# Token factors applied after the projections, and constant matmuls in four waits of TensorE

## The reference, cut to what matters

```
def rms_norm(x, g):
    y = xf * lax.rsqrt(jnp.mean(xf * xf, axis=-1, keepdims=True) + EPS)
    return (y * g.astype(jnp.float32)).astype(x.dtype)

def conv_ffn(h, w_up, conv_w, conv_b, w_down):      # h = rms_norm(x, g)
    gu = h @ w_up
    g, u = gu[..., :D_FF], gu[..., D_FF:]
    g = conv(g, conv_w) + conv_b                     # causal, width 3, per feature
    return (jax.nn.silu(g) * u) @ w_down

# keys and values: rms_norm(x, norm_kv) @ kv_w; queries: rms_norm(x, norm_mix[1]) @ w_q
```

## Time and profile before

| | |
|---|---|
| median of 3 runs | 2296.23 us (2291.31 to 2297.32) |
| the profiled execution | 2288.34 us, span in the profile 2286.5 us |
| PE busy | 2167.1 us (95%) |
| DVE, ACT, POOL busy | 56%, 33%, 30% |
| mean granted clock of PE | 0.963 |
| glu tiles on PE | until about 257 us |
| up and down of layer 0 | to 642 us |
| keys, values, queries | 650 to 788 us |
| stick-breaking attention, wo | 793 to 958 us |
| up and down of layer 1 | to 1335 us |

### The profile page before, as it was taken

One profiled execution on the slowest core, in us unless ns is written; L12 is line 12 of the kernel. 1 busy time (PEld: TensorE's weight loads), 2 busy tenths in 40 slices (PEclk: granted clock), 3 DMA queues, 4 the chain that ended last, 5 costly groups with the idle time before them and its releaser, 6 DMA issues. The chain is left out here.

```text
span 2286.5 us, 27572 instructions
## 1 busy us (share of the span) xinstructions
PE 2167.1 (95%) x10821; PEld 1584.2 (69%) x10821; DVE 1282.6 (56%) x2330; ACT 754.4 (33%) x1091; POOL 695.6 (30%) x436
## 2 busy tenths in 40 slices
PE   8859899999999999999999999999999999999898
PEld 7858688888868766778888855436875446886663
DVE  8562389984363267278882032348763574225872
ACT  3422333222243476332232131325651332332210
POOL 6614344445435500344444410011000342441000
PEclk9979899999989999999999989998999979999999
DMA  4032244434434500234443320130002213322201
GB/s 180 7 54 86 74 141 144 147 119 133 123 92 125 129 1 1 83 115 150 141 138 92 92 116 25 56 74 21 2 1 93 92 67 132 96 92 92 74 19 74
DMA packets 54096, 199.69 MB, mean 87 GB/s; under 512 B 9929, under 2 KB 10105, under 8 KB 48751
## 3 DMA queue, kind: packets, MB, share of 16 engines
q1 hardware_dynamic: 37440, 148.53, 20.7%
q0 software_dynamic: 12800, 48.23, 6.5%
q10 hardware_dynamic: 3728, 1.18, 0.3%
HBM read 179.04 MB, written 10.49 MB: 83 GB/s over the span
## 5 line engine op out<-in xcount | busy, mean ns | idle before, releaser
L1505 POOL TENSOR_TENSOR w_lo<-raw,w_hi 128x1024 fp32r<-128x1024 f32 (+1 forms) x216 | 513.8, 2379 | 854.8 <-ACT w_hi L1138 854.6
L595 PE MATMUL psum<-h_hi,w_hi 128*128 128x512 f32 x1216 | 487.6, 401 | 7.3 <-ACT h_hi L1145 5.5
L596 PE MATMUL psum<-h_hi,w_lo 128*128 128x512 f32 x1216 | 479.5, 394 | 0.0
L1138 ACT ACTIVATE w_hi<-raw 128x1024 fp32r<-128x1024 f32 (+1 forms) x216 | 224.9, 1042 | 605.8 <-PE psum L600 395.4
L600 PE MATMUL psum<-h_lo,w_hi 128*128 128x512 f32 x1216 | 303.3, 392 | 0.0
L595 PEld LDWEIGHTS psum<-h_hi,w_hi 128*128 128x128 f32 x1216 | 231.0, 190 | 71.3 <-ACT h_hi L1145 14.2
L600 PEld LDWEIGHTS psum<-h_lo,w_hi 128*128 128x128 f32 x1216 | 230.5, 190 | 48.5
L596 PEld LDWEIGHTS psum<-h_hi,w_lo 128*128 128x128 f32 x1216 | 231.9, 191 | 45.8 <-issue 0.2
L464 PE MATMUL psum<-big,ring 128*128 128x512 f32 x480 | 209.1, 594 | 0.0
L464 PEld LDWEIGHTS psum<-big,ring 128*128 128x128 f32 x480 | 90.9, 190 | 113.9 <-issue 112.6
L642 PE MATMUL psum<-f_hi,w_hi 128*128 128x512 f32 x352 | 137.6, 391 | 0.0
(11 more groups left out here) (384 smaller groups left out, 3388.2 us busy)
## 6 DMA issues: line engine op xcount, KB each, us to landing
raw<-in_ffn_w_up SPq DMA_DIRECT2D x88, 512.0 KB, 3.7
raw<-in_ffn_w_down SPq DMA_DIRECT2D x32, 512.0 KB, 3.6
raw<-in_hy_in SPq DMA_DIRECT2D x32, 512.0 KB, 3.5
ffn_buf<-in_ada_w POOLq DMA_DIRECT2D x20, 512.0 KB, 5.0
sq<-in_ada_w POOLq DMA_DIRECT2D x20, 512.0 KB, 5.1
raw<-in_ssm_w_glu SPq DMA_DIRECT2D x16, 512.0 KB, 3.7
spec<-big SPq DMA_DIRECT2D x8, 1024.0 KB, 3.9
big<-spec POOLq DMA_DIRECT2D x8, 1024.0 KB, 5.1
```

Of the source, the lines that this page charges most:

```text
L595: pe.matmul(o, hi[:, k, :], h_of(k), start=k == 0, stop=False)
L596: pe.matmul(o, lo[:, k, :], h_of(k), start=False, stop=False)
L1138: act.activation(w_hi[:, (n % 2) * HALF:(n % 2) * HALF + w], raw[:, (n % 4) * HALF:(n % 4) * HALF + w], ACT.Copy).then_inc(S["w_hi"], 1)
L1505: pool.tensor_tensor(w_lo[:, at:at + w], raw[:, (n % 4) * HALF:(n % 4) * HALF + w], w_hi[:, at:at + w].bitcast(F32), ALU.subtract).then_in ...
```

## The change

The three norms ffn0, kv and ffn1 are taken apart. ACT writes the high part of gain times X as soon as a row of X is there (`gained`), and its square (`row`); DVE writes the low part (`rest`). The projection runs on these without the token factor. PE sums the squares of rows 0 to 6 ahead of the first tile, those of row 7 in the middle of tile 0, and spreads the factor in the middle of tile 1 (`factor`, `mid`). The factor R is then multiplied in where the results are read: the gate branch (into `ZR`), the down tiles (`DOWN_R`, then added to X), keys and queries (`KQ`), values (`R_COL`). In the up part ACT now waits for DVE's multiplication before it writes the base of the convolution; the high part of the gate moves from DVE to ACT (`gate_hi`), the low part one step later (`gate_lo`). In the last glu step the order of a split and the sigmoid is changed. The buffers move: ada blocks 20 to 27 now lie in `ffn_buf` rather than `Hb`, their loads wait until the last gate is done, and stand behind the third chunk of a down tile rather than the first. `keep_clock` adds matmuls of constants: 8 before `scores(0)`, 3 before the sums of norm nw0, and 3 before each of the spreads of final, nw0 and final2.

```diff
-        ADA_ISSUE = [{2 * j: j for j in range(ADA_UP)} | {2 * FT + 3 * m: ADA_UP + m for m in range(KT)},
+        ADA_ISSUE = [{2 * j: j for j in range(ADA_UP)} | {2 * FT + 3 * m + 2: ADA_UP + m for m in range(KT)},
...
-                Hb[:, (j % 2) * HALF:(j % 2 + 1) * HALF]
+                ffn_buf[:, (j % 2) * HALF:(j % 2 + 1) * HALF]
...
+            def keep_clock(n, bank=None):
+                b = turn[0] % 8 if bank is None else bank
+                if n and last_release[b]:
+                    pe.wait_ge(*last_release[b])
+                for _ in range(n):
+                    pe.matmul(psum[:, b, 0:256], mat("ident"), mats[:, 0:256], start=True, stop=True)
+
+            def sums(name, ks):
+
+                o = take(pe, ("norm", name)) if ks[0] == 0 else ps(("norm", name))
+                for k in ks:
+                    pe.wait_ge(S["sq_ready"], n_sq[0] + 1)
+                    n_sq[0] += 1
+                    for j in range(4):
+                        i = pe.matmul(o[32 * j:32 * j + 32, 0:P], mat("ones")[:, 0:32],
+                                      sq_of(name, k)[:, j * P:(j + 1) * P], start=k == 0, stop=k == KT - 1,
+                                      skip_group_check=True)
+                    if name == "kv" and k < KT - 1:
+                        i.then_inc(S["sq_used"], 1)
+                if ks[-1] == KT - 1:
+                    fills(i, ("norm", name))
+
+            def factor(name):
+                def mid(t):
+                    if t == 0:
+                        sums(name, (KT - 1,))
+                    if t == 1:
+                        if name == "kv":
+                            o = take(pe, ("rc", name))
+                            pe.wait_ge(S["rn_ready"], WIDE_NORMS.index(name) + 1)
+                            fills(pe.transpose(o[:, 0:P], rows_of(name), mat("ident")), ("rc", name))
+                        spread(name)
+                return mid
...
             def norm(name):
 
                 src, n, m, _ = norm_src(name)
+                keep_clock(3 if name == "nw0" else 0)
...
-                norm(f"ffn{l}")
+                sums(f"ffn{l}", range(KT - 1))
...
+                    if mid:
+                        mid(t)
...
                         ada_turn(j)
+                    if l == 0 and m == 4:
+                        sums("kv", range(4))
...
+                    keep_clock(8, 7)
                     pe.wait_ge(S["masks_ready"], 2)
...
+            def gained(name, k):
+                act.activation(H_PARTS[name][0][:, k, :], X[:, k, :], ACT.Copy, scale=col(name, k)).then_inc(S["h_hi"], 1)
+
+            def row(name, k):
+                x_wait(k)
+                gained(name, k)
+                if name == "kv" and k >= 4:
+                    act.wait_ge(S["sq_used"], n_used[0] + k - 3)
+                act.activation(sq_of(name, k), X[:, k, :], ACT.Square).then_inc(S["sq_ready"], 1)
+
+            def root(name):
+                act.preload_act_table_set("sqrt_and_others")
+                act.wait_ge(*full(("norm", name)))
+                frees(act.activation(rows_of(name), ps(("norm", name))[:, 0:P], ACT.Sqrt, bias=eps, scale=1.0 / D),
+                      ("norm", name))
+                n_x[0] += 8
+                n_used[0] += 7 * (name == "kv")
...
-                for n in (2 * m + 2, 2 * m + 3):
-                    split_hi(n)
+                split_hi(2 * m + 2)
+                if m < 7:
+                    split_hi(2 * m + 3)
                 if m >= 2:
                     act.wait_ge(*free(("glu", 2 * (m - 2))))
                 evac(("glu", 2 * m + 1), scr[:, (m % 2) * L:(m % 2 + 1) * L], func=ACT.Sigmoid)
+                if m == 7:
+                    split_hi(2 * m + 3)
+                if m:
+                    row("ffn0", m - 1)
+            row("ffn0", 7)
...
-                    act.wait_ge(*full((f"up{l}", 2 * m)))
-                    act.activation(CONVG[:, m % 2, :], ps((f"up{l}", 2 * m)), ACT.Identity,
+                    act.wait_ge(*free((f"up{l}", 2 * m)))
+                    act.activation(CONVG[:, m % 2, :], ZR[:, m % 2, :], ACT.Identity,
                                    bias=col(f"conv{l}", 3 * FT + m), scale=col(f"conv{l}", 2 * FT + m)) \
                         .then_inc(S["conv_base"], 1)
                     split_hi(n0 + 2 * m + 2)
+                    if m >= 2:
+                        gate_hi(m - 2)
                     if m >= 1:
                         silu(m - 1)
                     split_hi(n0 + 2 * m + 3)
+                gate_hi(FT - 2)
                 silu(FT - 1)
+                gate_hi(FT - 1)
...
                 if j == ADA_UP:
-                    pool.wait_ge(*full(("up0", 2 * FT - 1)))
+                    pool.wait_ge(S["lo_done"], FT)
...
+            def rest(name, k):
+                hi, lo = H_PARTS[name]
+                dve.wait_ge(S["h_hi"], SPLIT_AT[name] + k + 1)
+                STT(lo[:, k, :], X[:, k, :], col(name, k), hi[:, k, :].bitcast(F32), ALU.mult, ALU.subtract) \
+                    .then_inc(S["h_lo"], 1)
...
+                    if factor:
+                        if m:
+                            dve.wait_ge(S["x_ready"], factor + m)
+                        step(TT(DOWN_R, ps(key), R, ALU.mult))
+                        own()
+                        i = TT(X[:, m, :], DOWN_R, X[:, m, :], ALU.add)
...
+            def factor(name):
+                inv_rms(name)
+                if name == "kv":
+                    frees(dve.tensor_copy(R_COL, ps(("rc", name))[:, 0:P:32]), ("rc", name))
+                keep_r(name)
+                dve.wait_ge(*free(("rb", name)))
...
                 for m in range(FT):
                     key = (f"up{l}", 2 * m)
-                    g, z = CONVG[:, m % 2, :], ps(key)
-                    dve.wait_ge(S["conv_base"], FT * l + m + 1)
+                    g, z = CONVG[:, m % 2, :], ZR[:, m % 2, :]
                     dve.wait_ge(*full(key))
-                    step(STT(g[:, 1:L], z[:, 0:L - 1], col(f"conv{l}", FT + m), g[:, 1:L], ALU.mult, ALU.add))
-                    own()
-                    frees(STT(g[:, 2:L], z[:, 0:L - 2], col(f"conv{l}", m), g[:, 2:L], ALU.mult, ALU.add), key)
-                    if m >= 1:
-                        gate(m - 1)
+                    if m >= 2:
+                        dve.wait_ge(S["conv_done"], FT * l + m - 1)
+                    frees(TT(z, ps(key), R, ALU.mult), key)
                     if m < ADA_UP:
                         if m >= 2:
                             ada_reduce(ADA_UP1 * l + m - 2)
                         ada_sum(ADA_UP1 * l + m)
+                    dve.wait_ge(S["conv_base"], FT * l + m + 1)
+                    step(STT(g[:, 1:L], z[:, 0:L - 1], col(f"conv{l}", FT + m), g[:, 1:L], ALU.mult, ALU.add))
+                    own()
+                    STT(g[:, 2:L], z[:, 0:L - 2], col(f"conv{l}", m), g[:, 2:L], ALU.mult, ALU.add) \
+                        .then_inc(S["conv_done"], 1)
+                    if m >= 1:
+                        gate(m - 1)
+                    if m >= 2:
+                        gate_lo(m - 2)
+                gate_lo(FT - 2)
                 gate(FT - 1)
+                gate_lo(FT - 1)
```

More of the change, by code:

```diff
@@ L1246, in ffn @@
                     split_hi(n0 + 2 * m + 3)
+                gate_hi(FT - 2)
                 silu(FT - 1)
+                gate_hi(FT - 1)
                 for n in range(n0 + 2 * FT + 2, n0 + HALVES):
                     split_hi(n)
+                    m = (n - n0 - 2 * FT) // 3
+                    if l == 0 and (n - n0 - 2 * FT) % 3 == 2 and m:
+                        row("kv", m - 1)
             ffn(0)
-            norm("kv", ready=x_wait, then=HALVES_AT["k"])
-            split_rows("kv")
+            split_hi(HALVES_AT["k"])
+            row("kv", 7)
+            split_hi(HALVES_AT["k"] + 1)
+            root("kv")
             for t in range(8):
-                key = ("k", t)
                 split_hi(HALVES_AT["k"] + t + 2)
-                split_rows("mix1", (t,), QHI)
-                act.wait_ge(*full(key))
+                gained("mix1", t)
+                act.wait_ge(*free(("k", t)))
                 for h in (2 * t, 2 * t + 1):
-                    act.activation(KS[half(h), h, :], ps(key)[half(h), :], ACT.Copy).then_inc(S["ks_hi"], 1)
+                    act.activation(KS[half(h), h, :], KQ[t % 2][half(h), :], ACT.Copy).then_inc(S["ks_hi"], 1)
             for q in range(8):
@@ L1300, in _ @@
                 split_hi(HALVES_AT["wo"] + t + 2)
-            n_x[0] += 8
+                if t:
+                    row("ffn1", t - 1)
+            split_hi(HALVES_AT["ffn1"])
+            row("ffn1", 5)
+            row("ffn1", 6)
+            split_hi(HALVES_AT["ffn1"] + 1)
+            row("ffn1", 7)
             ffn(1)
@@ L1965, in _ @@
                         own()
+            for t in range(8):
+                dve.wait_ge(*full(("k", t)))
+                if t >= 2:
```

(6 more changed lines are left out.)

183 lines of the change are left out of this document (96 added, 87 removed).

## The result

The change makes the kernel slower: 2388.38 us (median of four runs, 2385.30 to 2390.34) against 2293.77 (2290.16 to 2297.32), a ratio of 1.0411, 95% interval 1.0389 to 1.0434. I had forecast 2312, slower, with a range up to 2330. The direction is right, the size is not: +94.6 us where the sum had +15.9. The time of before is taken anew beside each experiment and lies between 2291.8 and 2293.8, so a difference between two groups of runs is good to about 2 us.

The account below looks back on a forecast made before the run. PE, busy 95% of the span, was taken as the bound. Gains of 28.7 us against a down-tile loss of 44.6 gave +15.9 on 2296.2, so 2312.1 us, range 2276 to 2330.

Parts of the forecast that it names:

- The direction: Whole kernel: slower, chance 0.66, against same 0.14 and faster 0.20.
- the sum: Whole kernel: loss of 44.6 us less gains of 28.7, so +15.9 us.
- The up tiles of layer 0: Up pairs: base, split and `w_lo` one DVE multiplication later, covered by DVE's slack; cost 0, up to 22 us without cover.
- rival 4: Up tiles: DVE's multiplication over 0.5 us late, PE waits up to 0.5 in 44 pairs; 2334 us, chance 0.06.
- The last sentence of the prediction: Prediction is wrong if L623 has no idle, or if even up tiles wait for `w_lo` all along.
- The down tiles of layer 0: Ada loads 9.1 us later: eight PE waits before the ada transposes, 32.6 us plus 12.0 of clock, loss 44.6.
- Rival 3: Down tiles of layer 0: every wait paid at half clock, loss 51.8 us, total +23.1, 2319 us; chance 0.15.
- kv: Norm before keys and values: cost falls from 15.6 to 4.5 us, gain 11.1.
- ffn1: Norm ahead of layer 1's up tiles: gain 6.6 us, or 4.2 after 2.4 of clock loss.
- The new wait at up tile 2: Tile 2's split stands behind the base, which waits for R: PE idles 4.0 us in ffn0 and in ffn1.
- ffn0: Norm ahead of layer 0's up tiles: tile 2 starts at 276.8, gain 10.0 us, or 7.6 after clock loss.
- Constant matmuls: They fill PE's waits at the opening and nw0: gains 3.3 us (0 to 6.2) and 2.5 us (0 to 5.2).

Follow-up runs that it names:

- the thinned kernel: Changed kernel with seven of eight products left out of the ada sums beside layer 0's up tiles: 2320.20 us.
- The fastest kernel: Changed kernel with product in PSUM, ada loads 21 to 27 early, next even tile's split ahead of R in every pair, sums between convolution and gate: 2262.75 us.

## Why the prediction was wrong, step by step

- **The up tiles of layer 0: cost 0, cover VectorE's slack.** This is the step that failed. I counted the durations of single instructions, found that VectorE loses a CAST and gains a shorter multiplication, and gave 0, at most 22 us (rival 4). I followed what waits for what, and left out what runs beside what: the sums, moved ahead of the convolution, began just before the split, and a split of 2.40 us became one of 5.3. The stretch is 76 us longer than the sum had it, and thinning the sums gives 68.2 back. Without them a cost near 0 was right: with the longer way to the split and the product in place, the thinned kernel loses 0.2 us a pair. The last sentence of the prediction named the sign, even up tiles that wait for `w_lo` all along, and that is what came. The rows to see it with were there. In the kernel before, the CAST reads and writes SBUF and takes 1.48, from 328.98 to 330.46, where the split beside it ends at 330.18; where no split runs beside it the same CAST takes 0.50 in that very trace, and it took 0.45 at the end of a split in the kernel before with its sums moved. I took 1.48 for its length and booked it as relief. And the multiply-adds of `ada_sum` in down tile 1 took 5.35 where an undisturbed chain takes 3.76, with a split inside it.

The Trainium skill, "SBUF — State Buffer", section "Who interferes with whom", states such a rule: a VectorE instruction with two SBUF inputs, or a copy, cast or `tensor_scalar` in a 2-port mode, and a GpSimd instruction that reads SBUF take one lock, and whichever is second stands still for the other's whole instruction. The runs agree, 2.40 to 5.32 on one side and 0.75 to 2.72 on the other, and no stall of a multiply-add with an input in PSUM. They go beyond it in one point: a split that was second waited not for one instruction of 0.34 us but for the rest of the dense chain (the table above).

- **The down tiles of layer 0: +44.6.** Right in place, number and total. Eight waits of 31.0 us where 32.6 stood; the traces give +46 for the stretch. Undoing the shift of seven loads gives 36.2: 27.3 of waits and 8.9 of clock (12.3 by the traces), 1.3 to 1.8 a wait, where I had 12.0 for all eight. The delay of the load minus the margin of each tile was the right working. How the waits spread over the tiles was wrong: I had more in the first four, whose sums have 16 instructions, and less in the last four with 8. They are 3.7 in each of the first four and 4.6, 4.6, 4.6 and 2.5 in the last. The seven multiply-adds there let the split in and stand still for it, one of them for 2.3 us instead of 0.35:

```profile
689.69 4.25 DVE L1957 SCALAR_TENSOR_TENSOR ffn_buf<-ffn_buf,small 128x128 f32<-128x128 f32 x6
...
690.68 2.34 POOL L1599 TENSOR_TENSOR w_lo<-raw,w_hi 128x1024 fp32r<-128x1024 f32 x1 [1.68 <-ACT w_hi L1193]
```

- **Rival 3, every wait paid at half clock.** At this case's 2.4 each that is 16.8 for the seven waits, and 8.9 to 12.3 came. The Trainium skill, "TensorE: Matmul & The Clock Gate", section on HAM oscillation, by which each round of such a loop starts throttled, holds here in part: the clock fell in the down tiles (0.91), but the price was lower.
- **kv: -11.1.** The traces give -11.5.
- **ffn1: -4.2.** The traces give -4.7 for all of layer 1's ffn. The new wait at up tile 2 is 4.08 us, predicted 4.0.
- **ffn0: -7.6, wait of 4.0 at up tile 2.** The wait is 6.67, and tile 2 starts at 280.28 and not at 276.8, against 286.8 before. Of the 2.7 above the forecast, 2.3 are the same fault: with the sums behind the gate the wait is 4.37. The wait itself, an order of ScalarE's queue, was read rightly: with the split ahead of the wait for R it is gone in both layers, though tile 4 takes over a part of it in layer 0 (2.5) and layer 1 (1.5).
- **Constant matmuls: -3.3 and -2.5.** Together they bring 3.6 by the comparison without them, which is not clear of noise. The norms give 1.9; at the opening the traces show 0.4, so there the bound of half the clock's loss was no guide and the lower bound, 0, was nearer.
- **The total without the three faults.** By the prediction's terms the gains without both waits at tile 2 are 11.1 + 14.0 + 10.6 + 5.8 = 41.5, less the first ada wait (3.7 + 2.4): 35.4. The fastest kernel brings 30.7.
- **The direction.** It holds by the down tiles and not by luck: the thinned kernel, in which the forgotten cost is nearly gone, is still slower than before (2320.20).
- **The range.** It held rival 4 at 0.5 us a pair, as if a hand-over of 0.73 were the largest thing that could happen to the split. It was 2.9 late for a reason no rival had.

Not resolved: from the end of layer 1 to the end of the kernel the changed kernel's trace is 3.8 us longer than before's (955.0 for 951.2), though the norms there are shorter. This may be nothing: the kernel before with its sums moved, which is the same there, has 954.8, and the other traces lie between 951.7 and 959.2.

## What to carry to other kernels

When an operation moves in one engine's queue, look not only at who waits for it, but at what will run at the same time on VectorE and GpSimd, and whether both read SBUF. A duration in a trace may hold a neighbour's work: compare it with the shortest one of the same kind and shape before it is booked as a cost or a gain. Where the two must overlap, put the operations that read PSUM beside GpSimd's work (here the product with R, written back to its bank, and the convolution): the same change went from 4% slower to 1.2% faster by order and place alone (sums, loads, split and product).

## What the runs showed of the hardware that I had not expected

- A GpSimd `tensor_tensor` on SBUF of 2.40 us that begins 1.27 us or more into a dense chain of 14 VectorE multiply-adds on SBUF (one each 0.26 us, the next begun before the last has ended) waits for the end of the chain, not of one instruction, in 149 of 152 cases; up to 0.84 us after the chain's start it runs at once and the chain stands still, in 44 of 44. In a chain of seven with 0.035 us of idle time between them it ran at once in 284 of 284. Why the first microsecond of a dense chain is different, and the three exceptions, no run here shows.
- VectorE's multiply-add with both inputs in SBUF rose from 0.75 to 2.72 us when a split was first; with one input in PSUM it stayed at 0.75 beside a running split. The `tensor_scalar` on 128 columns, two in 0.47, took 2.40 to 2.55.
- Idle times of TensorE of 2.47 us in each pair of tiles cost clock as well: it stayed at 1.00 for the first of them (295 to 350 us) and was 0.89 in the mean from 352 to 567 us, where a pair lasted 15.3 us rather than 13.9. With idle times of 1.25 us in the kernel before with its sums moved it stayed at 1.00.
